# Down projection of sixteen experts with tokens as result rows instead of channels, in a diffusion trunk kernel

## What is computed

```python
def expert_choice_ffn(h, w_router, w_gate, w_up, w_down):
    cap = EC_CAPACITY_FACTOR * N // N_EXPERTS            # 128 sample tokens, 16 prompt tokens
    aff = jax.nn.softmax((h @ w_router).astype(jnp.float32), axis=-1)
    gate, idx = lax.top_k(jnp.swapaxes(aff, 1, 2), cap)
    xs = jax.vmap(lambda hb, ib: hb[ib])(h, idx)
    hid = jax.nn.silu(einsum("becd,edf->becf", xs, w_gate)) * einsum("becd,edf->becf", xs, w_up)
    ys = einsum("becf,efd->becd", hid, w_down) * gate[..., None]
    return zeros((N, D)).at[idx].add(ys)                 # then x = x + g2 * this
```

## Time and profile before

| what | value |
|---|---|
| median of 3 runs | 2902.19 us (2900.83 to 2903.74) |
| the profiled execution | 2900.69 us, of which 2898.7 us are its span |
| TensorE matmul busy | 2594.7 us, 90% of the span |
| mean granted TensorE clock | 0.943 |
| DMA | 480.64 MB, 166 GB/s |
| the two expert loops | about 1018 to 1471 us and 2419 to 2871 us |

### The profile page before, as it was taken

The page is one execution under the profiler, slowest core; times in us unless marked ns, Lnnn a source line. Parts: engine busy times, 40 slices in busy tenths (PEclk is TensorE's granted clock), DMA queues, the critical chain, the costliest instruction groups (busy, mean ns, idle before and its releaser), DMA issues.

```text
span 2898.7 us, 43360 instructions
## 1 busy us (share of the span) xinstructions
PE 2594.7 (90%) x16540; PEld 1919.9 (66%) x16540; DVE 1300.1 (45%) x2726; ACT 625.3 (22%) x1298; POOL 656.8 (23%) x740
## 2 busy tenths in 40 slices
PE   3999989999899399999969998999999946999994
PEld 1555666665555199999935566566655525999993
DVE  2455545556775612222125554555577753222222
ACT  1233322112111012121123332221221101121121
POOL 0000013444542011221100000444464401122111
PEclk8999999999899599999989999999999977999997
DMA  8433331212542867787743333211144354778764
GB/s 284 154 103 104 101 127 57 82 70 82 199 149 95 290 225 264 267 299 266 237 153 104 102 116 115 92 63 71 65 180 157 123 193 154 272 262 292 278 238 147
DMA packets 223147, 480.64 MB, mean 166 GB/s; under 512 B 26318, under 2 KB 78238, under 8 KB 220574
## 3 DMA queue, kind: packets, MB, share of 16 engines
q1 hardware_dynamic: 205502, 422.12, 41.0%
q0 software_dynamic: 11264, 37.76, 5.1%
q10 hardware_dynamic: 6240, 18.87, 1.8%
HBM read 395.07 MB, written 83.64 MB: 165 GB/s over the span
## 4 chain that ended last, share of the span: by engine, by line
PE 78%; DVE 9%; issue 3%; DMA 3%; SPq 3%; ACT 2%; POOL 1%; POOLq 1%; DVEq 0%; ACTq 0%; PEldq 0%
PE bank L813 22%; PE bank L846 17%; PE bank L857 9%; PE bank L820 7%; PE bank L784 6%; PE bank L906 6%; DVE work L1522 5%; PE bank L1010 3%; ACT work L1225 2%; PE bank L921 1%; PE bank L1144 1%; PE bank L1061 1%; SPq L499 1%; PE bank L800 1%; DMA work<-x_d 1%
## 5 line engine op out<-in xcount | busy, mean ns | idle before, releaser
L813 PE MATMUL bank<-work 128*128 128x512 f32 (+1 forms) x1728 | 738.0, 575 | 24.3 <-ACT work L1225 13.9
L813 PEld LDWEIGHTS bank<-work 128*128 128x128 f32 x1728 | 319.1, 192 | 341.6 <-issue 303.5
L1225 ACT ACTIVATE work<-bank 128x256 f32<-128x256 f32 (+6 forms) x716 | 285.4, 432 | 1080.9 <-PE bank L846 318.4
L846 PE MATMUL bank<-work 128*128 128x144 f32 x4096 | 511.9, 288 | 2.2 <-DVE work L1522 2.2
L846 PEld LDWEIGHTS bank<-work 128*128 128x128 f32 x4096 | 508.2, 191 | 3.0 <-issue 2.4
L1522 DVE TENSOR_TENSOR work<-work 128x256 f32<-128x256 f32 (+3 forms) x629 | 361.6, 603 | 189.7 <-PE bank L1010 103.3
L784 PE MATMUL bank<-cst,work 128*128 128x128 f32 (+3 forms) x1888 | 250.7, 282 | 161.5 <-DVE work L1973 51.0
L784 PEld LDWEIGHTS bank<-cst,work 128*128 128x128 f32 (+3 forms) x1888 | 210.5, 143 | 207.2 <-DVE work L1973 51.5
L1225 ACT ACTIVATE work<-work 128x256 f32<-128x256 f32 (+3 forms) x247 | 169.0, 685 | 806.2 <-DVE work L1522 492.7
L1522 DVE TENSOR_TENSOR work<-bank,work 128x144 f32<-128x144 f32 (+2 forms) x218 | 90.1, 420 | 507.2 <-ACT work L1225 500.0
L906 PE MATMUL bank<-work 128*128 128x512 f32 x576 | 257.8, 601 | 5.0 <-ACT work L1225 3.0
(11 more groups left out here) (153 smaller groups left out, 2144.7 us busy)
## 6 DMA issues: line engine op xcount, KB each, us to landing
work<-in_w_gate_dram SPq DMA_DIRECT2D x32, 2048.0 KB, 8.4
work<-in_w_up_dram SPq DMA_DIRECT2D x32, 2048.0 KB, 13.4
work<-in_w_down_dram SPq DMA_DIRECT2D x32, 2048.0 KB, 10.1
work<-in_w_ada_dram SPq DMA_DIRECT2D x32, 1024.0 KB, 5.9
work<-sum_d SPq DMA_DIRECT2D x18, 1024.0 KB, 5.1
work<-in_w_ada_dram SPq DMA_DIRECT2D x8, 2048.0 KB, 13.2
work<-in_w_in_dram SPq DMA_DIRECT2D x8, 2048.0 KB, 15.9
hT_d<-work SPq DMA_DIRECT2D x18, 512.0 KB, 3.4
```

Of the source, the lines that this page charges most:

```text
L813: mm = pe.matmul(bank[:, bk, 0:w.shape[-1]], h[:, ch, :], w[:, ch, :], start=(ch == 0), stop=(ch == DC - 1))
L846: mm = pe.matmul(bank[:, 4 + f, o:o + CAP_S + CAP_P], w[:, ch, f * P:(f + 1) * P], e_xt[:, ch, :], start=(ch == 0), stop=(ch == DC - 1))
L1225: return act.activation(out, in_, func, **kw)
```

## The change

The down product swaps its operands: the hidden tokens are stationary and the weights move. The 128 sample tokens give two groups of four products of 512 columns (banks 3 and 7). The 16 prompt tokens give sixteen products of 256 columns into bank 6, one quarter of the channels in each of four column groups (partitions 32g to 32g+15). The result has tokens as rows, so the transposes, `take_down` and the tile `e_yt` go. `weighted` reads banks 3, 6 and 7; its prompt part is one 128 x 256 operation against `e_gq`, a quartered copy of the gate row that GpSimd makes before phase 5 ends. The prompt result leaves by four indirect DMAs of 16 rows x 1 KB, to an `x_d` seen as quarter rows, with row numbers made in phase 5 (`k_row`); they are issued ahead of the sample scatter. The waits move too: `down` waits for the hidden blocks one by one, and `gate_up` for `weighted` at f = 2 instead of f = 3.

```diff
+                for f in range(FC):                       # gate_up
-                    if f == 0:
-                        pe.wait_ge(sem["e_yt"], before("e_yt", n))
-                    if f == 3:
+                    if f == 2:
                         pe.wait_ge(sem["e_y"], before("e_y", n))
...
-            def down(n, m, p, next_n):
-                pe.wait_ge(sem["e_h"], by("e_h", n))
+            def down(n, m, p):
                 pe.wait_ge(sem[f"e_d{p}"], by(f"e_d{p}", m))
-                for ch in range(DC):
+                def token_rows(bk, c0):
                     for f in range(FC):
-                        o = (ch % 3) * (CAP_S + CAP_P)
-                        mm = pe.matmul(bank[:, DOWN_BANK[ch // 3], o:o + CAP_S + CAP_P], e_wd[p][:, f, ch * P:(ch + 1) * P], e_h[:, f, :],
+                        pe.wait_ge(sem["e_h"], by("e_h", n, f + 1))
+                        mm = pe.matmul(bank[:, bk, :], e_h[:, f, 0:CAP_S], e_wd[p][:, f, c0:c0 + 512], start=(f == 0), stop=(f == FC - 1))
+                    mm.then_inc(sem["e_dn"], 1)
+
+                token_rows(3, 0)
+                for f in range(FC):
+                    for g in range(4):
+                        mm = pe.matmul(bank[32 * g:32 * g + CAP_P, 6, 0:Q], e_h[:, f, CAP_S:], e_wd[p][:, f, Q * g:Q * (g + 1)],
                                        start=(f == 0), stop=(f == FC - 1))
-                    if ch % 3 == 2 or ch == DC - 1:
-                        mm.then_inc(sem["e_dn"], 1)
-                pe.wait_ge(sem["e_xta"], by("e_xta", next_n))
-                pe.wait_ge(sem["e_xtd"], by("e_xtd", next_n))
-                for ch in range(DC):
-                    if ch % 3 == 0:
-                        pe.wait_ge(sem["e_yt"], by("e_yt", n, ch // 3 + 1))
-                    mm = turn(bank[:, ch // 4, (ch % 4) * P:(ch % 4 + 1) * P], e_yt[:, ch, 0:CAP_S])
-                    if ch % 4 == 3:
-                        mm.then_inc(sem["e_bk"], 1)
-                for ch in range(DC):
-                    mm = turn(bank[0:CAP_P, 2 + ch // 4, (ch % 4) * P:(ch % 4 + 1) * P], e_yt[:, ch, CAP_S:])
-                mm.then_inc(sem["e_bk"], 1)
+                mm.then_inc(sem["e_dn"], 1)
+                token_rows(7, 512)
...
-            def take_down(n):                             # ScalarE, three copies out of PSUM
...
+                dve.scalar_tensor_tensor(out=e_yp[:, 0:Q], in0=bank[:, 6, 0:Q], scalar=e_g[:, 1:2],
+                                         in1=e_gq, op0=ALU.mult, op1=ALU.mult).then_inc(sem["e_y"], 1)
...
+                dve.tensor_copy(apart(k_t[:, 0, :]), thrice(k_v))      # phase 5, one copy
...
+                for g in range(4):                                     # phase 5, last
+                    dve.tensor_scalar(k_row[0:CAP_P, g, :].bitcast(U32), k_s[0:CAP_P, 1, 64:64 + NE], 4.0, float(g), ALU.mult, ALU.add)
...
+                for g in range(4):                                     # GpSimd, after barrier 4
+                    pool.tensor_copy(e_gq[32 * g:32 * g + 32, :], gate_row[32 * g:32 * g + 32, 1, 0, Q * g:Q * (g + 1)])
...
+                    pool.wait_ge(sem["e_y"], by("e_y", n, 2))
+                    quarters = x_d.rearrange("t (g c) -> (t g) c", g=4)
+                    for g in range(4):
+                        pool.indirect_dma_start(quarters, bass.IndirectOffsetOnAxis(ap=k_jp[0:CAP_P, g:g + 1].bitcast(U32), axis=0),
+                                                e_yp[32 * g:32 * g + CAP_P, 0:Q], None, compute_op=ALU.add).then_inc(sem["e_scp"], 16)
                     pool.wait_ge(sem["e_y"], by("e_y", n))
                     pool.indirect_dma_start(x_d, bass.IndirectOffsetOnAxis(ap=k_j[:, 0:1].bitcast(U32), axis=0), e_y, None, compute_op=ALU.add)
-                    pool.indirect_dma_start(x_d, bass.IndirectOffsetOnAxis(ap=k_j[0:CAP_P, 1:2].bitcast(U32), axis=0), e_yp[0:CAP_P, :], None, compute_op=ALU.add)
```

More of the change, by code:

```diff
@@ L321, in trunk @@
         s_diag = [v.rearrange("p (a b) -> p a b", b=P) for v in (r_gy, r_xn, r_junk)] + [r_ht]
-        DOWN_BANK = (3, 6, 7)
+        Q = D // 4
         take = carve(DC * (512 + 512 + 272))
@@ L336, in trunk @@
         e_yp = take(D)
-        e_yt = take(DC, CAP_S + CAP_P)
-        aff_t = e_yt.rearrange("p a b -> p (a b)")[0:LISTS, 0:512]
+        e_gq = e_yp[:, Q:2 * Q]
+        aff_rows = take(1024)
+        aff_t = aff_rows[0:LISTS, 0:512]
         k_v = take(P)[0:LISTS, :]
@@ L345, in trunk @@
         k_idx = take(2, NE)
+        k_row = take(4, NE)
+        k_jp = take(4)
         k_val = take(2, NE)
@@ L1212, in _ @@
                         turn_rows(n + 1)
-                        down(n, m, p, n + 1)
+                        down(n, m, p)
                 gate_up(l * NE + NE - 1, (l + 1) * (NE // 2), 0)
                 turn_rows(l * NE + NE)
-                down(l * NE + NE - 1, (l + 1) * (NE // 2), 0, l * NE + NE)
+                down(l * NE + NE - 1, (l + 1) * (NE // 2), 0)
                 gate_up(l * NE + NE, (l + 1) * (NE // 2), 1)
-                down(l * NE + NE, (l + 1) * (NE // 2), 1, l * NE + NE)
+                down(l * NE + NE, (l + 1) * (NE // 2), 1)
                 barrier(pe, l, 6)
@@ L1403, in silu_gate @@
                     ev(e_sg[:, f, :], bank[:, 4 + f, 0:CAP_S + CAP_P], ACT.Silu).then_inc(sem["e_sg"], 1)
-            def take_down(n):
[L1406 to L1410, removed]
             def squares_o(l, j):
@@ L1750, in weighted @@
                 dve.tensor_copy(e_g[:, 0:1], k_val[:, 0, bass.ds(e, 1)])
-                dve.tensor_copy(e_g[0:CAP_P, 1:2], k_val[0:CAP_P, 1, bass.ds(e, 1)]).then_inc(sem["e_gc"], 1)
+                dve.tensor_copy(e_g[:, 1:2], k_val[:, 1, bass.ds(e, 1)]).then_inc(sem["e_gc"], 1)
                 dve.wait_ge(sem["e_gc"], by("e_gc", n))
                 dve.wait_ge(sem["e_jc"], by("e_jc", n))
[L1754 to L1761, removed]
+                dve.wait_ge(sem["e_dn"], by("e_dn", n, 1))
+                dve.scalar_tensor_tensor(out=e_y[:, 0:512], in0=bank[:, 3, :], scalar=e_g[:, 0:1],
+                                         in1=gate_row[:, 1, 1, 0:512], op0=ALU.mult, op1=ALU.mult).then_inc(sem["e_y"], 1)
+                dve.wait_ge(sem["e_dn"], by("e_dn", n, 2))
+                dve.scalar_tensor_tensor(out=e_yp[:, 0:Q], in0=bank[:, 6, 0:Q], scalar=e_g[:, 1:2],
+                                         in1=e_gq, op0=ALU.mult, op1=ALU.mult).then_inc(sem["e_y"], 1)
+                dve.wait_ge(sem["e_dn"], by("e_dn", n))
+                dve.scalar_tensor_tensor(out=e_y[:, 512:D], in0=bank[:, 7, :], scalar=e_g[:, 0:1],
+                                         in1=gate_row[:, 1, 1, 512:D], op0=ALU.mult, op1=ALU.mult).then_inc(sem["e_y"], 1)
             def spread(k0, g0, sc, sh):
```

17 lines of the change are left out of this document (10 added, 7 removed).

## The result

The changed kernel took 2891.59 us in the median of 6 runs (2888.01 to 2893.7), the kernel before 2901.64 in its 6; the ratio is 0.9966, with a 95% interval of 0.9954 to 0.9977. A second series of five rounds gave 0.9956 (0.9944 to 0.9968). So the change is faster, by 10 us in the first series and 13 in the second, where 22 were forecast. The direction holds and 2891.6 lies in the upper part of the forecast's 2866 to 2896, but the gain is less than half of the forecast in the first series and 60% of it in the second.

What follows compares the result with a forecast made beforehand. TensorE's issued work was taken to bound the expert loops. Terms of -25.0 (down product), -1.4 (last expert), +3.8 (loop ends) and +0.5 (phase 5) summed to -22.1, giving 2880.1 us; range 2866 to 2896.

Steps and rivals of the forecast that it cites:

- The new TensorE work: Down product per expert: 6.87 sample, 2.00 prompt, 0.10 passage, sum 8.97 us against 9.75; -25.0 us for 32 experts.
- The 2.00: Prompt product's term per expert: 32 matmuls at L792's 0.0625 us each, 2.00 us.
- the full overlap's 1.72: Lower bound for the prompt product per expert: 32 matmuls of 0.2147 us overlapping by four, 1.72 us.
- The last expert's wait: Each layer's last expert, before down: 0.7 us of TensorE idle time goes, twice, -1.4 us.
- GpSimd in the loop: Expert loop: five scatters end 0.62 us later than today's last; the gather's slack falls from 2.2 to 1.6, hidden.
- one of the signs of being wrong: Expert loop: TensorE idle before `turn_rows` for a gather would show the forecast wrong; no size given.
- Ends of the loops: After each layer's last expert: sample scatter issued at 4.56 us, landing 6.1 later; +1.9 twice, +3.8 us.
- Phase 5: Added copy and four small VectorE operations that make the row numbers: +0.5 us, between 0 and 1.7.
- the first rival: Prompt product: column groups do not overlap, 32 matmuls take 6.87 us, about 3036 us in all; chance 3%.
- Unhidden loads: Prompt product: weight loads of 90 ns set a floor of 2.88 us, about 2908 in all; chance 5%.
- GpSimd was not late: Loop rival: quarter scatters above about 1.75 us each make the gather late; at 2.0 each, 2918 us; chance 5%.
- The case of switches between forms that drain more than 0.10: Down product: at 0.4 us each way the gain falls to 0.1 per expert, about 2902 us; chance 5%.

Runs made afterwards that it cites:

- e1: Changed kernel with one more GpSimd drain in every scatter after the first, right after the wait for the previous scatters' landing; 2872.89 us, ratio 0.9897.
- e4: Changed kernel as it is, profiled once more; 2889.68 us in a single run.
- e5: Changed kernel as it is, timed in five rounds beside the kernel before; 2888.65 us, ratio 0.9956.
- e7: Changed kernel with a drain in every scatter and the prompt result written by one indirect DMA of 128 quarter rows; 2868.93 us, ratio 0.9884.
- e8: e7 with the prompt products after both sample halves and the sample scatter ahead of the prompt scatter; 2861.78 us, ratio 0.9858.
- e3: Changed kernel with the prompt products issued group by group, the same 32 matmuls; 2976.84 us in a single run.

## Why the prediction was off, step by step

- **The new TensorE work**: right, sum and mechanism. Forecast 8.97 us per expert, measured 9.02 at the same place. Inside it the terms are shared out differently. The prompt product is eight rounds of 0.216, 1.73 us, near the full overlap's 1.72. The 2.00 had taken L792's 1.00 twice, and with it L792's way out of the column groups twice. The way in costs 0.09, for a forecast 0.10. The way out costs 0.22: the last round lasts 0.11 longer and the next full-width matmul 0.10 longer. The sum also lacked 0.10 for the first 512-column matmul behind the transposes, which the kernel before paid as well. That piece shows beside the last expert, which has no transposes ahead (3.52 to the prompt product, where the others take 3.63):

```profile
2832.50 3.60 PE L857 MATMUL bank<-work 128*128 128x512 f32 x8
2836.02 1.92 PE L863 MATMUL bank<-work 128*16 128x256 f32 x32
```

  The Trainium skill (TensorEngine Tiling (Array Packing), Key Properties) names such a drain at a change of tiling mode without a size; here in and out together cost 0.31 us.
- **The last expert's wait**: the 0.7 us of idle time went, as forecast. The loops are 13.3 us shorter each, where 12.5 + 0.7 were forecast. That this agrees so well is in part luck. The first expert of a loop took 27.7 to 29.8 us by where the clock stood, which moved the pair in favour of the change by 1.1 and 0.4 us, and other pairs of profiles have 11 to 14.
- **GpSimd in the loop**: right in its times (first scatter at G - 2.1, sample scatter at G + 4.4, both within 0.2). What it missed is a landing. In the first layer's last but one expert the gather is issued as always, 8.41 us into `gate_up`. But loads for the next layer, which take 21 us, start 6 us before that expert's first gather, and this gather landed 8 us after issue, where the forecast had at most 5.4 from the second loop. TensorE idled, one of the signs of being wrong that the prediction had named, though for the landing and not for GpSimd:

```profile
1403.97 1.69 PE L787 MATMUL bank<-cst,work 128*128 128x128 f32 x16 [0.59 <-DMA work<-xn_d,work]
```

  The same wait stands in e1, e4 and e5 (0.4 to 0.9 us) and not in e7 and e8, whose gathers are issued earlier.
- **Ends of the loops**: this is the step that failed. The prediction priced issue and landing and got them (the sample scatter issued 4.1 us after TensorE's last matmul and 6.2 to land, for a forecast of 4.56 and 6.1). It put at nothing any change behind the last landing, without a reason. There stands a drain of 5.29 us that grows by 0.082 for each indirect DMA in the whole loop. Three more scatters in each of 16 experts are 48 x 0.082 = 3.93, in each layer: 7.9 us that the term of +3.8 lacked. The rest of each end's growth, 5.8 - 3.93 = 1.9 us, is what was forecast. With the drain the sum is -14.2, and the parts of the two profiles give -15.1.
- **Phase 5**: 0.1 to 0.6 us in the second layer, by how much of the growth around it one counts (0.2 ahead of the selection, 0.3 in it, 0.1 behind it), for a forecast 0.5.
- **Outside the loop**: no term stood for it. In the first pair of profiles the mixing phases of the two layers differ by +7 us in all, mostly through clock dips in unchanged code. Of the 12 us that the first series missed the forecast by, the drain is 7.9; the other 4 (1 in the second series) stay open between chance and a small shift that the runs don't separate.
- **The rivals**: the groups did overlap, but e3 shows how near the first rival lay: it needed only the loop order turned around. Unhidden loads did not come, and GpSimd was not late. The case of switches between forms that drain more than 0.10 named the wrong drain: they cost 0.31 in all, not 0.4 each way, and its 2902 was nearer to the time than its reason deserved.

## What to carry to other kernels

Small products in four column groups are worth it when the groups cycle from matmul to matmul; price a round of four at what one of its matmuls takes alone, and add the passage in and out. Count the indirect DMAs that a change adds over a whole phase, not only those on the path at its end, because GpSimd's next drain pays for each; a drain put in its idle time takes the bill away, and here it took 16 to 19 us off the changed kernel, more than the change itself had brought. Such a drain also waits for a gather on the way, so it needs idle time for that. A piece of the chain whose length nobody has explained is not a constant.

## What the runs showed of the hardware that was not expected

- GpSimd's drain takes 0.05 us plus 0.082 us per indirect DMA since its last one, when all of them have landed (2, 5, 64 and 112 DMAs). With a gather on the way it ends 0.20 to 0.50 us after the gather has landed, and lasted 1.4 to 3.8 us.
- 32 matmuls of 256 columns with 16 stationary columns: 1.85 us with groups cycling, 4.47 us group by group. Matmuls of one group start 0.216 us apart in both orders; four groups that cycle start 7 ns apart.
- From 512-column matmuls of full width into column groups 0.09 us is lost, and 0.22 on the way back.
- An accumulating scatter of 16 rows of 1 KB takes GpSimd 1.27 to 1.41 us (median 1.30), as long as the 16 rows of 4 KB before (1.32 to 1.36); one of 128 rows of 1 KB takes 1.58 to 1.65, and one of 128 rows of 4 KB 1.55 to 1.64. The number of DMAs costs it time, and the number of rows a little; the bytes of a row don't show.
- The places of TensorE's clock dips change from one execution of a kernel to the next, which moved 930 us of unchanged work by 3 us between two profiles of the kernel before, and by 4.4 among three of the changed one.
